# The second layer's work on columns 12 to 591 of 592, from the gated branch on

## The reference, cut to what matters

```
x = concat(meta[16], x_prompt[512])            # and x_sample [8 x 8], same weights
layer 0: m = retention + HGRN heads(x) @ w_out_ab
layer 1: gate, r = split(x @ w_in_c)           # r: conv of width 4, then a recurrence over all tokens
         h = linear recurrence(conv4(r))       # h[t] needs every earlier token
         m = (gelu(gate) * h) @ w_out_c
each layer: x = LN(alpha*x + m)
            u, v = split(x @ w_up)             # 2 x 2816
            x = LN(alpha*x + (gelu(conv3(u)) * v) @ w_down)
y_prompt = x[16:]                              # the 16 learned tokens are dropped
also returned: states after the last token, the last 2 columns of u per sequence, the last 3 of r
```

## Time and profile before

| | us |
|---|---|
| median of 3 runs (lowest, highest) | 1471.12 (1470.57, 1471.30) |
| the profiled execution, as timed | 1473.63 |
| its span, first to last instruction | 1471.8 |
| PE busy | 1432.6 (97%) |
| DVE, ACT, POOL busy | 838.2, 620.1, 72.8 |

### The profile page before, as it was taken

One profiled execution on the slowest core, in us unless ns is written; L12 is line 12 of the kernel. 1 busy time (PEld: TensorE's weight loads), 2 busy tenths in 40 slices (PEclk: granted clock), 3 DMA queues, 4 the chain that ended last, 5 costly groups with the idle time before them and its releaser, 6 DMA issues.

```text
span 1471.8 us, 24538 instructions
## 1 busy us (share of the span) xinstructions
PE 1432.6 (97%) x10256; PEld 1402.5 (95%) x10256; DVE 838.2 (57%) x1265; ACT 620.1 (42%) x1010; POOL 72.8 (5%) x96
## 2 busy tenths in 40 slices
PE   7999999999999999999999999999999999999995
PEld 7999999989999999999999899998999999999995
DVE  4656665645755644534555787877555455245555
ACT  4443535443644233312342676736431343133434
POOL 0010101000300000000000400004000000000000
PEclk9999999999999999999999999999999999999998
DMA  7131322323231322222223122121323222222222
GB/s 265 58 118 59 83 80 82 94 85 119 83 96 63 101 72 87 86 86 74 74 85 96 35 86 72 58 83 47 101 61 98 80 79 86 87 73 86 73 72 82
DMA packets 37231, 125.24 MB, mean 85 GB/s; under 512 B 4352, under 2 KB 6528, under 8 KB 36864
## 3 DMA queue, kind: packets, MB, share of 16 engines
q1 hardware_dynamic: 32976, 111.42, 24.3%
q0 software_dynamic: 2560, 8.91, 2.2%
q10 hardware_dynamic: 1584, 3.33, 0.7%
HBM read 115.96 MB, written 7.70 MB: 84 GB/s over the span
## 4 chain that ended last, share of the span: by engine, by line
PE 92%; DVE 3%; ACT 3%; issue 1%; DMA 0%; POOL 0%; ACTq 0%; POOLq 0%; DVEq 0%; SPq 0%
PE PS L555 28%; PE PS L556 28%; PE PS L557 28%; PE PS L804 1%; PE PS L723 1%; PE PS L714 1%; PE PS L729 1%; PE PS L673 1%; PE PS L694 1%; DVE Y L1457 1%; DVE Y L1469 1%; PE PS L703 0%; PE PS L660 0%; PE PS L707 0%; DMA raw<-weights 0%
## 5 line engine op out<-in xcount | busy, mean ns | idle before, releaser
L555 PE MATMUL PS<-xhi,whi 128*128 128x296 f32 x2176 | 664.5, 305 | 14.8 <-DVE wlo L1196 7.8
L556 PE MATMUL PS<-xlo,whi 128*128 128x296 f32 x2176 | 653.7, 300 | 0.0
L557 PE MATMUL PS<-xhi,wlo 128*128 128x296 f32 x2176 | 651.1, 299 | 0.0
L555 PEld LDWEIGHTS PS<-xhi,whi 128*128 128x128 f32 x2176 | 411.5, 189 | 22.3 <-POOL xlo L547 9.0
L556 PEld LDWEIGHTS PS<-xlo,whi 128*128 128x128 f32 x2176 | 411.6, 189 | 1.4
L557 PEld LDWEIGHTS PS<-xhi,wlo 128*128 128x128 f32 x2176 | 410.9, 189 | 0.0
L555 PE MATMUL PS<-hhi,whi 128*128 128x296 f32 x912 | 276.1, 303 | 3.9 <-ACT S L1140 2.7
L556 PE MATMUL PS<-hlo,whi 128*128 128x296 f32 x912 | 274.7, 301 | 0.0
L557 PE MATMUL PS<-hhi,wlo 128*128 128x296 f32 x912 | 273.9, 300 | 0.0
L1189 DVE TENSOR_TENSOR wlo<-raw,whi 128x1024 fp32r<-128x1024 f32 (+1 forms) x195 | 235.3, 1209 | 53.8 <-ACT whi L838 49.4
L838 ACT ACTIVATE whi<-raw 128x1024 fp32r<-128x1024 f32 (+1 forms) x195 | 203.0, 1043 | 136.9 <-PE PS L557 71.2
(11 more groups left out here) (227 smaller groups left out, 1225.7 us busy)
## 6 DMA issues: line engine op xcount, KB each, us to landing
raw<-weights SPq DMA_DIRECT2D x182, 512.0 KB, 3.5
raw<-weights SPq DMA_DIRECT2D x16, 384.0 KB, 3.0
Y<-xT ACTq DMA_DIRECT2D x8, 296.0 KB, 3.9
yT<-Y SPq DMA_DIRECT2D x16, 148.0 KB, 1.8
C<-consts SPq DMA_DIRECT2D x1, 2146.5 KB, 13.1
S<-s_hgrn POOLq DMA_DIRECT2D x4, 512.0 KB, 4.6
S<-s_ret POOLq DMA_DIRECT2D x4, 512.0 KB, 5.9
hgrn_out<-S POOLq DMA_DIRECT2D x4, 512.0 KB, 4.8
```

The costliest lines, as they stand in the source:

```text
L555: pe.matmul(dst, wh, h, start=first, stop=False)
L556: pe.matmul(dst, wh, lo, start=False, stop=False)
L557: return pe.matmul(dst, wl, h, start=False, stop=last)
```

## The change

Columns 0 to 11 (`DEAD` = 12) are left out from the "g" units on. The remaining 580 columns are two halves of 290, starting at columns 12 and 302, where before they were two of 296 starting at 0 and 296. The "r" units, the convolution, the recurrence and everything before keep all 592 columns. In bytes of a row the two halves start at 48 and 1208, before at 0 and 1184. No instruction is added, removed or moved: every engine has the same instructions in the same order, with fewer columns each. 3936 matmuls of `products` go from 296 to 290 columns: 8 "g" units x 48, 8 units of U_OUTC x 48, 44 up units x 48, and 8 down units x (6 + 8 + 8) input tiles x 6. So do 12 fp32 matmuls of the moments of ln 2 and ln 3. On DVE and ACT the rows of 592 become 580, the pairs of rows 2 x 580, the convolved rows 596 for 608. Two rows are cleared over 14 columns for 2 (L1503). The 16 stores of the result have 290 columns each.

```diff
+DEAD = META - 4
+def off(u):
+    return 0 if u < U_RNN or (u < U_OUTC and MIXER[u - U_RNN][0] == "r") else DEAD
+def wid(u):
+    return (T - off(u)) // 2
...
+        def off_ln(ln):
+            return DEAD if ln > 1 else 0
...
-        def span(half):
-            return slice(half * HT, half * HT + HT)
+        def span(half, at=0):
+            w = (T - at) // 2
+            return slice(at + half * w, at + half * w + w)
...
-                    sp.dma_start(yT[m * P:m * P + P, span(half)], Y[:, m, span(half)]).then_inc(y_out, 16)
+                    sp.dma_start(yT[m * P:m * P + P, span(half, DEAD)], Y[:, m, span(half, DEAD)]).then_inc(y_out, 16)
...
-                            t = slice(half * HT, half * HT + HT)
-                            mm = products(a[:, half, 0:HT], high(u + i)[:, cols], low(u + i)[:, cols],
+                            t = span(half, off(u + i))
+                            mm = products(a[:, half, 0:wid(u + i)], high(u + i)[:, cols], low(u + i)[:, cols],
                                           hi[:, k, t], lo[:, k, t], k == 0, k == n - 1)
...
-                    mm = pe.matmul(PS[:, 4 + 2 * i, 0:HT], const("mean_d"), s(Z0 + i, 0, HT), start=True, stop=True)
+                    mm = pe.matmul(PS[:, 4 + 2 * i, 0:wid_ln(ln)], const("mean_d"), s(Z0 + i)[:, span(0, off_ln(ln))],
+                                   start=True, stop=True)
...
-                        done(act.activation(r[:, FW - 1:FW - 1 + HT], a[:, 0, 0:HT], ACT.Copy))
+                        done(act.activation(r[:, FW - 1 + at:FW - 1 + mid], a[:, 0, 0:wid(u)], ACT.Copy))
...
-                done(act.activation(halves(pair(GEL, m % 2)), acc[u % 2][:, :, 0:HT], ACT.Gelu_apprx_tanh),
+                done(act.activation(halves(pair(GEL, m % 2)[:, DEAD:]), acc[u % 2][:, :, 0:wid(u)], ACT.Gelu_apprx_tanh),
                      free[u % 2], u // 2 + 1)
...
-                done(act.activation(hhi[:, 2 * p:2 * p + 2, :].rearrange("p a b -> p (a b)"), pair(GEL), ACT.Copy), r_hi)
+                done(act.activation(hhi[:, 2 * p:2 * p + 2, DEAD:], by_row(GEL)[:, :, DEAD:], ACT.Copy), r_hi)
...
-                    done(dve.memset(S[:, r, 0:FW - 1], 0.0), pads if r else None)
+                    done(dve.memset(S[:, r, 0:FW - 1 + at], 0.0), pads if r else None)
...
-                done(tt(pair(GEL), pair(SCAN), pair(GEL), ALU.mult), hmul)
+                live = by_row(GEL)[:, :, DEAD:]
+                done(tt(live, by_row(SCAN)[:, :, DEAD:], live, ALU.mult), hmul)
```

More of the change, by code:

```diff
@@ L415, in pair, with by_row @@
             return two if j is None else two[:, j * T:(j + n) * T]
+        def by_row(i):
+            return pair(i).rearrange("p (a t) -> p a t", a=2)
         def at_row(n):
@@ L526, in second_half_sums @@
                 n = 0
+                cols = span(1, off_ln(ln))
                 for i in range(2):
@@ L535, in second_half_sums @@
                             pool.wait_ge(half_sums, 4 * ln + n - 1)
-                        pool.tensor_tensor(s(z)[:, span(1)], s(z)[:, span(1)], row[:, span(1)],
+                        pool.tensor_tensor(s(z)[:, cols], s(z)[:, cols], row[:, cols],
                                            ALU.add).then_inc(half_sums, 1)
@@ L595, in half_product @@
                     pe.wait_ge(y_half, 6 * third + 3)
-                dst = acc[u % 2][:, half, 0:HT] if third is None else PS[:, 5, 0:HT]
+                dst = acc[u % 2][:, half, 0:wid(u)] if third is None else PS[:, 5, 0:wid(u)]
+                t = span(half, off(u))
                 mm = products(dst, high(u)[:, cols], low(u)[:, cols],
-                              hi[:, k, span(half)], lo[:, k, span(half)], k == 0, k == n - 1)
+                              hi[:, k, t], lo[:, k, t], k == 0, k == n - 1)
                 if k == n - 1 and half:
@@ L946, in squares @@
                 act.wait_ge(free[u % 2], u // 2 + 1)
-                done(act.activation(s(T0 + m % 2), Y[:, m, :], ACT.Square), sq_ok)
+                done(act.activation(s(T0 + m % 2, off(u)), Y[:, m, off(u):], ACT.Square), sq_ok)
             def layer_norm(ln, u):
                 which, layer = ("ffn" if ln % 2 else "mix"), ln // 2
+                w, at = wid_ln(ln), off_ln(ln)
                 def square(m, half):
@@ L972, in shifted @@
                         act.wait_ge(ln_c, (2 * ln + half) * KT + m + 1)
-                        y, b = Y[:, m, span(half)], par(f"ln_{which}_b", layer * KT + m)
+                        y, b = Y[:, m, span(half, at)], par(f"ln_{which}_b", layer * KT + m)
                         if ln == 3:
@@ L981, in shifted @@
                             slot_used(act, u + 2)
-                        act.activation(xhi[:, first:first + n, span(half)], Y[:, first:first + n, span(half)],
+                        act.activation(xhi[:, first:first + n, span(half, at)], Y[:, first:first + n, span(half, at)],
                                        ACT.Copy).then_inc(x_hi, 1)
@@ L1008, in ffn @@
                 ub = U_FFN0 if layer == 0 else U_FFN1
+                at, mid = off(ub), off(ub) + wid(ub)
                 act.wait_ge(pads, 2 * layer + 1)
@@ L1040, in ffn @@
                         act.wait_ge(conv, jj + 1)
-                        row = S[:, 2 + j % 2, 0:FU - FW + 1]
+                        row = S[:, 2 + j % 2, at:FU - FW + 1]
                         done(act.activation(row, row, ACT.Gelu_apprx_tanh), gel)
                         act.wait_ge(free[u % 2], u // 2 + 1)
-                        done(act.activation(hhi[:, j - first, :], s(4 + j % 2), ACT.Copy), h_hi)
+                        done(act.activation(hhi[:, j - first, at:], s(4 + j % 2, at), ACT.Copy), h_hi)
                     else:
@@ L1398, in add_tile @@
                     weights_lo(v)
-                a = acc[u % 2][:, :, 0:HT]
-                y = halves(Y[:, m, :])
+                a = acc[u % 2][:, :, 0:wid(u)]
+                y = halves(Y[:, m, off(u):])
                 if ln == 0:
@@ L1427, in add_half @@
                         dve.wait_ge(x_loaded[m], 32)
-                    y = Y[:, m, span(half)]
-                    a = PS[:, 5, 0:HT] if i == 2 else acc[(u + i) % 2][:, half, 0:HT]
+                    y = Y[:, m, span(half, at)]
+                    a = PS[:, 5, 0:w] if i == 2 else acc[(u + i) % 2][:, half, 0:w]
                     if half:
@@ L1462, in scaled @@
                     if ln == 3:
-                        y = Y[:, first:first + n, span(half)]
+                        y = Y[:, first:first + n, span(half, at)]
                         done(tt(y, y, over_rows(6 + half, n), ALU.mult))
```

71 lines of the change are left out of this document (38 added, 33 removed).

## The result

The changed kernel takes 1458.4 us (median of 4 runs, 1455.6 to 1458.8) against 1470.9 us before, a ratio of 0.9911 with a 95% interval of 0.9894 to 0.9928. Timed again, it gave 1456.4 us (median of 5 runs; a sixth, disturbed one of 7913 us is left out) against 1470.5, ratio 0.9910 (0.9895 to 0.9924). So the change is worth 12.5 to 14.1 us by the medians, clearly outside the 0.2% of no change, and more than the 9.7 us forecast. The profiled execution took 1458.78 us.

The account below looks back on a forecast made before the run. PE was taken to bound the kernel by how often it starts a matmul; 9.2 us from narrower matmuls plus 0.5 us from chains made 9.7 us, so 1471.12 - 9.7 = 1461.4 us, range 1458.2 to 1467.6.

Parts of the forecast that it names:

- The bound: Whole kernel: PE is busy 97% of the span; other engines matter only where PE waits for them.
- The worth of six columns, 2.5 ns: Matmuls cut from 296 to 290 columns: 2.5 ns less each, 9.2 us over the 3690 on the path.
- Rival C: Moving operands starting off multiples of 32 bytes cost extra per matmul: up to 11.4 us more, 1482.0 us; chance 0.05.
- The range's low end: Whole kernel: 2.76 ns per matmul, no half-clock drop, and 0.8 us for new operand places; 1458.2 us.
- Rival A: PE matmuls: loading the next weight sets the 136 ns, so columns give nothing; 1470.6 us; chance 0.07 in full.
- A in part: PE matmuls: loader and columns share the limit, 0.8 ns per matmul, 3.0 us; 1467.6 us with the chains; chance 0.05.
- The chains: ACT and DVE work off PE, ahead of 959 us, in two norms and at the end: narrower rows save 0.5 us.
- The recurrence stage: 850 to 942 us: PE never pauses, though DVE is busy 82% of it, 75.5 of 92 us.
- The wait at 956 us: PE's wait for the accumulator ahead of 959 us: grows from 2.74 to about 2.9 us, PE arriving 0.26 us earlier.
- B: Half clock behind the 956 us wait: may fail to come, 1.4 us less, 1460.0 us, chance 0.13; longer, chance 0.02.

Follow-up runs that it names:

- experiment 8: Kernel before with only the PE matmuls narrowed, other engines at all columns; 614.18 us from the changed stretch to the end, against 625.09 before and 612.74 changed.
- experiment 9: Changed kernel with the four operand tiles moved by 8 bytes; 1467.4 us in one run.
- 5: Changed kernel with the weight tiles (high and low) moved by 48 bytes; 134.4 ns mean spacing in the last ConvFFN, against 133.05 in the changed kernel.
- 6: Changed kernel with the four operand tiles moved by 48 bytes, weights not moved; 135.0 ns mean spacing in the last ConvFFN, against 133.05 in the changed kernel.
- 10: Changed kernel with the four operand tiles moved by 16 bytes; 134.4 ns mean spacing in the last ConvFFN, against 133.05 in the changed kernel.
- 15: Changed kernel with operand tiles moved by 48 bytes and later operands written 12 columns further to the front; 1455.3 us, ratio 0.9902 to the kernel before.

## Why the prediction was right or wrong

*The bound*: right. PE is the path in all but the stretches named, and PE alone carries at least 10.9 of the 12.35 us (experiment 8).

*The worth of six columns, 2.5 ns, with 0 and 2.76 as its bounds*: this is the step that failed, the term behind the 9.2 us. It measured 3.3 ns in the ConvFFN (136.4 to 133.05), outside both bounds. No run shows the 2.5 ns as the worth of six columns at full clock, nor the 2.76; both are estimates, half of the 5.0 ns at half clock and the share 6 x 136 / 296. They are two ways to divide 136 ns among 296 columns, with the place of the operand taken as one average, so that its change was put at nothing. The runs show what stood there instead: a width part of 1.4 ns at the old starts and a place part of 1.95 ns. Between the averages of nine places each at both widths (136.5 and 134.1; they are not the same nine) the width is worth 2.4 ns, and the changed kernel lies 1.05 ns under its average, the kernel before 0.1 under its own. So 2.5 ns was near what six columns are worth at an average place, and that the change landed on the best of the nine was luck. 3022 matmuls x 0.8 ns = 2.4 us of the missing 2.65 us are this term in the ConvFFN.

*Rival C* named the place, with the wrong sign as the only one that it priced: "if the new places all fell to 142 ns". The long stretches that agreed on one mean were taken as evidence that the place averages out. They only went through the same few places again, with all rows 2368 bytes apart and both halves at multiples of 32. The 138.3 ns of experiment 9 show that the bad side is real: that move of 8 bytes cost the first layer 1.9 ns a matmul (1467.4 us in one run). The range's low end allowed 0.8 us for new places, where the ConvFFN alone gained 2.4 us beyond the forecast.

*Rival A*, the loader: refuted, 117.0 ns at 256 columns. In the trace before, each load starts 0.01 us or less behind the matmul ahead (699.94 behind 699.93, 700.07 behind 700.07), which fits that. *A in part* (0.8 ns for six columns, 0.13 ns a column) falls by the same runs: 0.485 ns a column from 296 to 256, and the spread between places (at most 2.5 ns, 0.06 ns a column over 40 columns) is far too small to bridge that. No run shows the 0.8 ns of its sum; at 0.485 ns a column six columns are 2.9 ns, and the changed kernel gained 3.3.

*The chains*: forecast 0.5 us. The stretches in which they lie gave 0.33 us at the end, 0.29 around the norm and 0.06 in the wait ahead of 959 us, some of PE's share included. So the size is about right, but no run has them by themselves. The 2 x 2.5 ns of a moment's fp32 matmul is shown: those of the first half of both norms (L761 before, L787 after) start 248 to 249 ns apart with 296 columns and 243 to 244 with 290.

*The recurrence stage*: it gave 0.94 us, near the 0.98 of the prediction (288 and 102 matmuls x 2.5 ns), but by luck, as two errors that cancel: at 3.2 ns these 390 were worth 1.25 us, and 0.3 us was given back in a wait that the prediction did not have. PE now reaches the last gate before the convolution (L1654, DVE) is done, at 936.88 us. The first matmul of this gate in the changed kernel, with 0.36 us between two starts where 0.14 us was usual:

```profile
936.58 0.30 PE L582 MATMUL PS<-xhi,wlo 128*128 128x290 f32 x1
936.94 1.26 PE L832 MATMUL PS<-Y,S 128*128 128x296 f32 x4
```

The same place before:

```profile
940.04 0.30 PE L557 MATMUL PS<-xhi,wlo 128*128 128x296 f32 x1
940.18 1.19 PE L804 MATMUL PS<-Y,S 128*128 128x296 f32 x4
```

Before, the convolution (L1620) was done at 940.05 us, 0.13 us ahead of PE. "In the recurrence stage PE never pauses" was read from the busy share, which hides how close DVE is behind; 75.5 of 92 us was the warning.

*The wait at 956 us*: forecast to grow to 2.9 us, it shrank to 2.69, since PE had lost its lead at the last gate. From the last product ahead of that gate, the chain to the end of the wait became 0.09 us shorter (18.99 to 18.90 us; forecast 0.07), and PE's own way to the wait only 0.03 us (15.95 to 15.92) instead of 0.26. *B*: the half clock behind it stayed in both profiles of the changed kernel. It is missing in five variants with moved tiles (5, 6, 9, 10 and 15). The prediction was right to price it, and blind to the two other places ahead of the change, near 30 and 327 us, where the same happens or not from run to run. These moved the two profiled executions by 2.55 us against each other; taken as the change's, that would have made it 14.9 us. The three runs it started from lay within 0.7 us, where 14 later ones covered 5.7.

## What to carry to other kernels

In this kernel, bound by dense fp32r matmuls, the spacing of their starts at full clock depended on where weights and operands lie in SBUF as well as on their columns. The place was worth 2 to 2.5 ns of 136, as much as five or six columns. So where such matmuls bound a kernel, measure a few shifts of the tiles by 8 to 48 bytes, before and after any change that moves the operands, or its gain or loss is credited to the wrong cause. Compare two profiles from one place in the program to the same place, with equal counts of matmuls, and look at the granted clock ahead of the change first. And where PE is busy without a pause, see how close the engine behind it is: a faster PE can run into a wait that the trace before doesn't have (0.3 us at the last gate, 0.66 us in experiment 8).

## What the runs showed of the hardware that was not expected

- At full clock fp32r matmuls with a new weight each start 117.0, 128.9, 132.2, 133 to 135 and 135.8 to 138.3 ns apart at 256, 280, 288, 290 and 296 columns: 10 to 15 ns over an estimate of 0.417 ns a column, half of what a column took at half clock. At half clock they start 213.3, 240.0, 241.7 and 246.7 ns apart at 256, 288, 290 and 296 columns (0.833 ns a column), within 0.1 ns at every place that ran there.
- A move of all four operand tiles by 8 bytes changed 296-column matmuls from 136.4 to 138.3 ns, ones by 16 and 48 bytes to 135.8; one by 128 bytes turned the pattern over the tiles and kept the mean. Moving the weights by 48 bytes changed 136.4 to 136.1 and 133.05 to 134.4. What makes this was not separated.
- Ahead of the change identical instructions ran with or without a piece of half clock: 3.4 us near 30 and 10.2 us near 327 us in the profile before, 3.4 us near 31 and 321 us in that of the changed kernel, none in that of experiment 8. The 14 runs of the kernel before differ by 5.7 us, and their mean granted clock goes with it: 0.995 in those of 1468 us, 0.990 in those of 1473 us.
